# Rounding and splitting the weights of a two-layer encoder on two engines, in four one-unit slots

## What is computed

```python
def swiglu(h, w_gate, w_up, w_down):
    return (jax.nn.silu(h @ w_gate) * (h @ w_up)) @ w_down

def ffn_sublayer(x, w, mod, l, slot, j):
    h = modulate(x, w['norm_pre'][l, slot], mod[:, slot, 0], mod[:, slot, 1])
    y = swiglu(h, w['ffn_w_gate'][l, j], w['ffn_w_up'][l, j], w['ffn_w_down'][l, j])
    return add_branch(x, y, w['norm_post'][l, slot], mod[:, slot, 2], FFN_RES)
```

## Time and profile before

| | us |
|---|---|
| median of 3 runs | 3968.12 (3966.95 to 3969.39) |
| span of the profiled execution | 3966.7 |
| TensorE busy | 3697.3 |
| VectorE busy | 1991.0 |
| GpSimd busy | 2197.0 |

### The profile page before, as it was taken

One profiled execution on the slowest core, in us unless ns is written; L12 is line 12 of the kernel. 1 busy time (PEld: TensorE's weight loads), 2 busy tenths in 40 slices (PEclk: granted clock), 3 DMA queues, 4 the chain that ended last, 5 costly groups with the idle time before them and its releaser, 6 DMA issues.

```text
span 3966.7 us, 63424 instructions
## 1 busy us (share of the span) xinstructions
PE 3697.3 (93%) x26506; PEld 3441.6 (87%) x26506; DVE 1991.0 (50%) x2200; ACT 580.2 (15%) x1157; POOL 2197.0 (55%) x956
## 2 busy tenths in 40 slices
PE   6999999899999899999899999989889997999997
PEld 3999999778567899999789999978878777999997
DVE  5734636549533737356553443566765335322334
ACT  2000000321332200000210000042132123000001
POOL 3767767556003567667666777756600005777775
PEclk9999999899789999999899999989999658999998
DMA  5333323243001324223122232212300001222221
GB/s 204 136 108 111 136 101 118 78 107 131 7 22 43 106 97 144 106 106 140 64 95 101 105 113 100 101 56 75 79 9 1 1 1 54 85 87 93 85 85 65
DMA packets 80752, 342.75 MB, mean 86 GB/s; under 512 B 13960, under 2 KB 17544, under 8 KB 50936
## 3 DMA queue, kind: packets, MB, share of 16 engines
q1 hardware_dynamic: 36976, 248.02, 17.6%
q10 hardware_dynamic: 43656, 93.04, 7.3%
HBM read 329.93 MB, written 11.11 MB: 86 GB/s over the span
## 4 chain that ended last, share of the span: by engine, by line
PE 74%; issue 12%; POOL 6%; DVE 5%; ACT 2%; ACTq 1%; POOLq 0%; DVEq 0%
PE psum L578 61%; POOL w_lo L494 3%; POOL w_hi L491 2%; PE psum L562 2%; DVE arena L1532 1%; PE psum L1001 1%; PE psum L983 1%; PE psum L943 1%; PE psum L955 1%; PE psum L1004 1%; PE psum L1002 1%; PE psum L958 1%; ACTq L1141 1%; PE psum L545 1%; PE psum L616 1%
## 5 line engine op out<-in xcount | busy, mean ns | idle before, releaser
L491 POOL TENSOR_TENSOR w_hi<-raw,one_col 128x1024 fp32r<-128x1024 f32 x464 | 934.7, 2014 | 1682.9 <-PE psum L600 829.4
L578 PE MATMUL psum<-h_hi,w_hi 128*128 128x272 f32 x5120 | 1489.5, 291 | 21.9 <-POOL w_lo L494 16.1
L578 PE MATMUL psum<-h_hi,w_lo 128*128 128x272 f32 x5120 | 1481.5, 289 | 0.0
L578 PE MATMUL psum<-h_lo,w_hi 128*128 128x272 f32 x5120 | 1477.8, 289 | 0.0
L494 POOL TENSOR_TENSOR w_lo<-raw,w_hi 128x1024 fp32r<-128x1024 f32 x464 | 1221.2, 2632 | 36.4
L578 PEld LDWEIGHTS psum<-h_hi,w_hi 128*128 128x128 f32 x5120 | 965.2, 189 | 43.1 <-issue 42.0
L578 PEld LDWEIGHTS psum<-h_lo,w_hi 128*128 128x128 f32 x5120 | 965.4, 189 | 0.2 <-issue 0.2
L578 PEld LDWEIGHTS psum<-h_hi,w_lo 128*128 128x128 f32 x5120 | 964.5, 188 | 0.0
L578 PE MATMUL psum<-hid_hi,w_hi 128*128 128x272 f32 x2048 | 607.4, 297 | 0.6
L578 PE MATMUL psum<-hid_hi,w_lo 128*128 128x272 f32 x2048 | 600.1, 293 | 0.0
L578 PE MATMUL psum<-hid_lo,w_hi 128*128 128x272 f32 x2048 | 598.0, 292 | 0.0
(11 more groups left out here) (284 smaller groups left out, 3328.3 us busy)
## 6 DMA issues: line engine op xcount, KB each, us to landing
raw<-in_w_stream SPq DMA_DIRECT2D x232, 1024.0 KB, 4.8
arena<-in_ada_w ACTq DMA_DIRECT2D x72, 768.0 KB, 5.6
arena<-in_ada_w ACTq DMA_DIRECT2D x32, 384.0 KB, 4.3
spare<-in_ada_w ACTq DMA_DIRECT2D x5, 768.0 KB, 16.9
rel_spread<-arena ACTq DMA_DIRECT2D x1, 3072.0 KB
spare_h<-in_ada_w ACTq DMA_DIRECT2D x3, 768.0 KB, 15.7
x<-in_x_t SPq DMA_DIRECT2D x1, 2176.0 KB, 18.6
out_y_t<-x SPq DMA_DIRECT2D x1, 2176.0 KB, 7.0
```

The costliest lines, as they stand in the source:

```text
L491: pool.tensor_tensor(w_hi[:, u], raw[:, s, u], one_col[:].broadcast_to([P, D]), ALU.mult)\
L578: mm = pe.matmul(psum[:, 2 * u + b, 0:HT], a[:, u, w], m[:, k, t], start=(k == 0 and i == 0), stop=(k == KD - 1 and i == 2))
```

## The change

`raw`, `w_hi` and `w_lo` become four slots of one unit each, and `raw` is laid over `w_lo`: VectorE subtracts in place. SyncE loads single units (512 KB) and waits for the unit that used the slot. GpSimd does nothing but round, one copy per unit, in a straight line of 464. VectorE subtracts (`split_weight`), three units ahead of the one whose output it handles; the calls stand at fixed places of its program. All eight tiles of `add_branch` are VectorE's. The first block of a feed-forward copies into y, and y is no longer cleared. TensorE's loops run over two pairs, so that slot numbers are constants. The hunks left out do the same in further product loops, pass slot numbers and lay out the weights as single units.

```diff
-        raw = sb("raw", [P, 2, 2, D])
-        w_hi = sb("w_hi", [P, 2, D], F32R)
-        w_lo = sb("w_lo", [P, 2, D], F32R)
+        w_hi = sb("w_hi", [P, SLOTS, D], F32R)
+        w_at = nc.sbuf_base
+        w_lo = sb("w_lo", [P, SLOTS, D], F32R)
+        raw = nc.alloc_sbuf_tensor_at("raw", [P, SLOTS, D], F32, offset=w_at)
...
-                    sp.wait_ge(w_split, 4 * i - 2 + 2 * s)
-                    sp.dma_start(raw[:, s], io["w_stream"][2 * i + s]).then_inc(w_loaded[s], 16)
+                    sp.wait_ge(unit_done, SLOTS * i + s - SLOTS + 1)
+                    sp.dma_start(raw[:, s], io["w_stream"][SLOTS * i + s]).then_inc(w_loaded[s], 16)
...
+            for c in range(UNITS):
+                s = c % SLOTS
+                pool.wait_ge(w_loaded[s], 16 * (c // SLOTS) + 16)
+                pool.tensor_copy(w_hi[:, s], raw[:, s]).then_inc(w_rounded, 1)
...
+            def split_weight(c, kb=0):
+
+                if isinstance(kb, int) and c + kb * BLOCK_UNITS >= UNITS:
+                    return
+                s = c % SLOTS
+                dve.wait_ge(w_rounded, kb * BLOCK_UNITS + c + 1)
+                dve.tensor_tensor(w_lo[:, s], raw[:, s], w_hi[:, s].bitcast(F32), ALU.subtract).then_inc(w_split, 1)
...
             conditions(0)
+            for c in range(AHEAD):
+                split_weight(c)
...
                         dve.tensor_tensor(split(h32[:, j % 2]), split(silu[:, j % 2]), halves(2), ALU.mult)\
                             .then_inc(bank_free[1], 1)
+                        split_weight(2 * (n0 + j) + AHEAD, kb)
...
                         dve.tensor_tensor(hid_lo[:, j], h32[:, j % 2], hid_hi[:, j].bitcast(F32), ALU.subtract)\
                             .then_inc(hid_ready, 1)
+                        split_weight(2 * (n0 + j) + 1 + AHEAD, kb)
                         if ADA_PARTS[f]:
                             ada_step(ADA_CHUNKS_BEFORE[f] + kb, j, ADA_PARTS[f])
...
-                        dve.tensor_tensor(split(y[:, m]), split(y[:, m]), halves(2 * (m % 2)), ALU.add)\
-                            .then_inc(bank_free[m % 2], 1)
+                        if begins:
+                            op = dve.tensor_copy(split(y[:, m]), halves(2 * (m % 2)))
+                        else:
+                            op = dve.tensor_tensor(split(y[:, m]), split(y[:, m]), halves(2 * (m % 2)), ALU.add)
+                        op.then_inc(bank_free[m % 2], 1)
+                        split_weight(2 * (n0 + KD) + m + AHEAD, kb)
...
-                for i, k in enumerate(k for k in range(KD) if k not in POOL_TILES):
+                for k in range(KD):
                     dve.wait_ge(y_gated, KD * n + k + 1)
                     dve.tensor_tensor(y[:, k], y[:, k], rstd, ALU.mult).then_inc(y_scaled, 1)
...
+                for m in range(6):
+                    split_weight(2 * FIRST["ab_in"] + m + AHEAD)
                 dve.wait_ge(wi_ready, 1)
+                for m in range(6, SCORE_UNITS):
+                    split_weight(2 * FIRST["ab_in"] + m + AHEAD)
+                    for e in scores_after(m):
+                        add_score(e, *score_items()[e])
...
-                for _ in range(TOPK_P // 8):
+                for r in range(TOPK_P // 8):
+                    if r % 4 == 0:
+                        split_weight(2 * FIRST["ab_in"] + SCORE_UNITS + 4 * (i - 1) + r // 4 + AHEAD)
                     choose_eight(i)
...
             for m in range(QKV):
+                split_weight(first_unit + m + 2)
                 convolve(m)
+            split_weight(first_unit + QKV + 2)
             convolve_sample()
+            for m in range(QKV + 3, QKV + 7):
+                split_weight(first_unit + m)
             decay_rows()
             columns()
+            for m in range(QKV + 7, GDN_UNITS + 1):
+                split_weight(first_unit + m)
```

More of the change, by code:

```diff
@@ L259, in build @@
         out_stored = sem("out_stored")
-        w_loaded = [sem("w_loaded0"), sem("w_loaded1")]
+        w_loaded = [sem(f"w_loaded{s}") for s in range(SLOTS)]
         w_rounded = sem("w_rounded")
@@ L487, in _ @@
         def _(pool):
[L488 to L510, removed]
-                if b % 2:
-                    split_pair(b // 2, 0)
-            def add_branch(n):
-                pool.wait_ge(rstd_ready, 2 * n + 2)
-                for i, k in enumerate(POOL_TILES):
-                    pool.wait_ge(y_gated, KD * n + k + 1)
-                    pool.tensor_tensor(y[:, k], y[:, k], rstd, ALU.mult).then_inc(y_scaled_pool, 1)
-                    pool.wait_ge(y_scaled_pool, len(POOL_TILES) * n + i + 1)
-                    pool.tensor_tensor(x[:, k], x[:, k], y[:, k], ALU.add).then_inc(x_ready_pool, 1)
-            pool.wait_ge(w_loaded[0], 16)
-            for u in range(2):
-                split_unit(0, u, u)
-            done = 1
-            ends = [FIRST[name] + 1 for name in ("ab_in", "ffn1", "ffn2", "gdn_in", "ffn3")] + [PAIRS]
-            for n, end in enumerate(ends):
-                split_pairs(done, end)
-                done = end
-                add_branch(n)
+            for c in range(UNITS):
+                s = c % SLOTS
+                pool.wait_ge(w_loaded[s], 16 * (c // SLOTS) + 16)
+                pool.tensor_copy(w_hi[:, s], raw[:, s]).then_inc(w_rounded, 1)
         @block.tensor
@@ L565, in ada_total, with unit @@
                     mm.then_inc(ada_turned, 1)
-            def unit(u, n, hi, lo, ready=None, tail_ready=None):
+            def unit(u, n, at, hi, lo, ready=None):
+                slot = 2 * at + u
                 pe.wait_ge(w_split, 2 * n + u + 1)
@@ L666, in product @@
                     first_pair(first, hi, lo, ready)
-                with pe.Fori(first + bool(ready), first + pairs) as n:
-                    unit(0, n, hi, lo)
-                    unit(1, n, hi, lo)
+                n, end = first + bool(ready), first + pairs
+                if (end - n) // 2:
+                    with pe.Fori(0, (end - n) // 2) as i:
+                        for at in range(2):
+                            unit(0, n + 2 * i + at, (n + at) % 2, hi, lo)
+                            unit(1, n + 2 * i + at, (n + at) % 2, hi, lo)
+                if (end - n) % 2:
+                    unit(0, end - 1, (end - 1) % 2, hi, lo)
+                    unit(1, end - 1, (end - 1) % 2, hi, lo)
             def rel_bias():
@@ L1595, in ffn, with block_of @@
             def ffn(f, n0, n_norm):
-                def block_of(kb, last):
+                def block_of(kb, begins, ends):
                     q = KD * (KB * f + kb)
@@ L1619, in block_of @@
                                     ADA_PARTS[f])
-                        if last and m:
+                        if ends and m:
                             y_squares(n_norm, m - 1)
-                with dve.Fori(0, KB - 1) as kb:
-                    block_of(kb, False)
-                block_of(KB - 1, True)
+                block_of(0, True, False)
+                with dve.Fori(1, KB - 1) as kb:
+                    block_of(kb, False, False)
+                block_of(KB - 1, False, True)
                 y_squares(n_norm, KD - 1)
```

119 lines of the change are left out of this document (57 added, 62 removed).

## The result

The changed kernel takes 3923.34 us (median of four runs, 3917.02 to 3930.82), the kernel before 3968.76 in its four: a ratio of 0.9885, with a 95% interval of 0.9871 to 0.9900, or 45 us less. The forecast was 32 us less, 3936.

The account below looks back on a forecast made before the run. TensorE, busy for 93% of the span, was taken to bound the kernel, leaving its idle time and low clock to win. The terms -16 - 9 + 3 - 9.5 - 11 - 10 + 3.6 + 17 = -32 gave 3936 us, range 3898 to 3966.

Parts of the forecast that it names:

- The wait on GpSimd's split: Feed-forwards: TensorE's 16.1 us of waiting for GpSimd to split weights goes, -16 us.
- The ada stall: Behind a block's last gate/up pair, TensorE's wait on VectorE's adaptive-norm steps shrinks 4.1 to 3.0 us, eight times: -9.
- The clock falls stay: Behind those eight waits in the first two feed-forwards the clock still falls, 3.7 us each; none of 30 us returns.
- first rival: The clock holds in the shorter stalls before the small adaptive-norm products: 30 us more come back, 3906 us; chance 0.20.
- The third feed-forward: With half the adaptive-norm width, its stall grows from about 0.6 to 1.4 us, over four: +3 us.
- The sum of squares: At the end of a product, TensorE's wait of 5.5 us becomes 3.6, five of six times: -9.5 us.
- The residual add: All eight tiles on VectorE take 11.5 us instead of 12.7; 2 us at five places, 1.2 at the last: -11.
- The DeltaNet convolution: DeltaNet layer: waits of 4.3 and 2.4 us on ScalarE go, and one clock fall of 3.7: -10 us.
- The start: Three splits stand between the conditions and the first normalisation, for which TensorE waits: +3.6 us.
- The top-k: Before attention, twelve splits in VectorE's search delay the first mask-add: +17 us (+11 to +24).
- The second rival: GpSimd's copy takes 1.9 us and gets between VectorE's steps twice per last pair, stalls 5.5 us: 3978 us; chance 0.13.
- The third: Top-k costs +24 us, and convolution and residual adds give nothing (+21): 3964 us, within 0.2%; chance 0.11.

## Why the prediction came out as it did, step by step

The direction and the size hold (3923 for 3936, inside the range), but the sum was right by errors of both signs: the gains below were priced some 25 us too low, and against that stand a loss of 19 us that was not in the sum and a gain priced 5 too high. That they nearly cancel is luck.

- **The wait on GpSimd's split: -16, and it was about -23.** The list of waits understated it. Five of the seven distances between a block's gate/up pairs in the first two feed-forwards were 12.3 to 12.9 us; all are 12.11 in the changed kernel. Added up over eight blocks, and with 1.1 us in the first pair of each of the four feed-forwards, that is 23.5 us. The page's groups hint at the same: in front of the weight loads of these matmuls 42.0 us of idle time without a named cause before, 14.5 after.
- **The ada stall: -9, and -12.** The chain was 8.3 us, not 9.1: the copy cost 0.85 in it and not 1.3, and neighbouring steps overlap by some tenths that I had not taken off.
- **The clock falls stay: right in kind.** All eight did; three came in half the length, -5 that I hadn't counted (one of the eight before had cost 3.8). The first rival's full 30 us did not come. What a fall costs was 3.2 us rather than the 3.7 I took from the first.
- **The third feed-forward: +3, and 0.** Its waits are 3.3 us now and were 3.4.
- **The sum of squares: -9.5, and -9.6.** Right in size, with the wrong reason: I had put the split on the path, and ScalarE's table load and square are there.
- **The residual add: -11, and -17.** The mechanism holds: the run with this part alone brings 13, since the next normalisation also starts 1.4 us sooner behind the last tile. The other 4 are the memset of y, a term that the prediction had put at 0 as lying under ScalarE's and TensorE's work; at three of the five places the normalisation waited for it.
- **The DeltaNet convolution: -10, and about -5.** The 4.3 us on ScalarE did not go: the row is the same to the digit in every run, whatever VectorE and GpSimd did. The 2.4 us wait went, but not the clock fall behind it: the 32 small products there bring the clock to 0.50 without any wait in front, as these two rows of the changed kernel show (below). The stage shows -9.9 in all, since the sum of squares (-2) and a wait on ScalarE (12.8 to 10.0) are in it; that wait is 10.0 to 15.8 us in these kernels, whose program there is the same, so I don't count it.

```profile
2799.06 4.32 PE L824 MATMUL psum<-spare,arena 128*128 128x32 f32 x32
```
```profile
2802.00:2804.00 2.00, 2.00 (x10) 0.50 0.14 55
```

- **The start: +3.6, and +3.6.**
- **The top-k: +17, and +14.8.** By the named mechanism, in-order splits that wait for the unit which frees the slot, and then the splits themselves.
- **Not in the sum: +19 in the score units.** The step that failed is "a unit's copy is done 5.2 us after the slot's old unit, its split 6.4 us after". It rested on a load of 3.5 us as if each load had the DMA engines to itself, which is the median over the whole run (3.6) but not the time here, and I read the DMA share only in the feed-forwards. The page of the kernel before had the row: a 3072 KB transfer in ScalarE's queue, and the landing times in its stretch go up to 21.1 us. (The formula that the prediction draws on for 512 KB stands in the Trainium skill, SBUF — State Buffer, under § The DMA setup-cost knee and not under the section it names; with the queue alone the 3.5 to 3.6 us agree with its 3.2.)

The terms as measured add up to -36 of the -47.5 us between the two profiles. Of the rest 4.6 lie in the part of attention behind the first mask-add and 2.8 in the wait on ScalarE named above, both of which differ as much between runs of the same program there; for some 4 us I have no cause.

The second rival (slower, with the copy between VectorE's steps twice) fails on the copy's 1.17 us. The run with the multiply bears out half of it: a copy of 2.02 us costs 24 us and brings the clock down in the third feed-forward, but it met VectorE's steps once in a last pair and not twice, with stalls of 3.3 us instead of 5.5 and 3947 us instead of 3978. The third (the splits in order cost the gain) was the right kind of loss at the wrong place. No run takes the four one-unit slots without the subtract on VectorE, so what each of the two brings is not shown.

## What to carry over

When a wait moves to an engine that does other work, price what stands behind it in that engine's program at the worst latency of what it waits for, not at the median; where a large transfer shares the DMA engines, that was six times as long here (20.9 us for 3.5). Put such a step behind the work that others wait for and far enough ahead of its use; here five moves of the same instructions, one of them empty, were worth 78 us, more than the change itself. And read a stall's price from the spacing of the work, not from the list of waits alone.

## What the chip did that was not expected

The clock's fall depended on what surrounds a wait. In the run with both splits behind the ada steps, waits of 1.4 to 1.5 us with wide matmuls on both sides left it at 1.00; 1.3 us in front of twelve one-column products brought it to 0.50 each time, at a cost of 1.6 us in seven cases of eight; 0.4 us in front of them left it at 1.00 in all three cases. After 2.4 us it cost 3.2 us in five and 1.6 in three, after 4 us, in the kernel before and the run with the residual add alone, 3.0 to 3.8. In front of six such products, 1.6 to 1.7 us cost nothing once, 1.6 twice and 3.2 once.

And a VectorE step beside GpSimd's one-input copy was lengthened too, two ada steps by 0.85 us where the two-input multiply cost 1.7 (4.32 and 5.18 against 3.47). It was not spared, only held up for less. Nor do only VectorE's steps with two SBUF inputs wait, as the prediction had it. Between the multiply and the subtract of the earlier trace rows the kernel before has this cast, with one input:

```profile
180.44 1.46 DVE L1606 CAST hid_hi<-arena 128x544 fp32r<-128x544 f32 x1
```

It takes 1.46 us beside GpSimd's multiply, where the same shape takes 0.43 without GpSimd. The multiply in front of it, whose second input is in PSUM, takes its 0.72 us with GpSimd busy.
